# Expert weights in pieces of two experts with longer rows per partition, and TensorE working on two pieces at a time

## What is computed

```
for each layer of two:                       # w_gate, w_up: [16, 1024, 512], w_down: [16, 512, 1024]
    scores  = softmax(modulated(x) @ w_router)          # 256 tokens x 16 experts
    for each expert e:
        chosen = its 32 best tokens
        h      = silu(xs @ w_gate[e]) * (xs @ w_up[e])  # xs: the 32 chosen tokens, [32, 1024]
        y      = h @ w_down[e]                          # [32, 1024]
        x[chosen] += gate * weight * y
```

## Time and profile before

| | |
|---|---|
| runs | 1672.56, 1678.06, 1679.40 us; median 1678.06 |
| span of the profiled execution | 1675.7 us (its own time beside the span is not listed; the runs lie from 3.1 below to 3.7 above this span) |
| TensorE busy | 1557.6 us, 93% of the span |
| VectorE, ScalarE busy | 695.0 us, 347.3 us |
| HBM read | 438.51 MB, 262 GB/s over the span |
| mean granted TensorE clock | 0.979 of full |

### The profile page before, as it was taken

The page is one execution under the profiler, slowest core; times in us unless marked ns, Lnnn a source line. Parts: engine busy times, 40 slices in busy tenths (PEclk is TensorE's granted clock), DMA queues, the critical chain, the costliest instruction groups (busy, mean ns, idle before and its releaser), DMA issues.

```text
span 1675.7 us, 22597 instructions
## 1 busy us (share of the span) xinstructions
PE 1557.6 (93%) x9541; PEld 1123.0 (67%) x9541; DVE 695.0 (41%) x1635; ACT 347.3 (21%) x811; POOL 96.6 (6%) x113
## 2 busy tenths in 40 slices
PE   6998999999999999999999999999999999996656
PEld 3785788888776788888887878744544776842212
DVE  2334377777416378877433134402212334310011
ACT  3144310000114330010124243310010334211100
POOL 0003200000002310000011102000000002000000
PEclk8999999999999999999999999899999999998988
DMA  9568579996583268669363244499999444789997
GB/s 354 175 232 284 207 278 352 344 341 244 195 241 124 86 219 310 233 247 335 127 226 111 73 151 178 175 403 409 409 409 397 174 151 168 283 349 409 409 409 306
DMA packets 167705, 441.02 MB, mean 263 GB/s; under 512 B 7690, under 2 KB 19636, under 8 KB 167604
## 3 DMA queue, kind: packets, MB, share of 16 engines
q1 hardware_dynamic: 166800, 439.12, 70.4%
q10 hardware_dynamic: 804, 0.45, 0.1%
HBM read 438.51 MB, written 1.05 MB: 262 GB/s over the span
## 4 chain that ended last, share of the span: by engine, by line
PE 77%; DMA 11%; issue 3%; ACT 3%; POOL 2%; PEld 1%; DVE 1%; SPq 1%; ACTq 0%; PEldq 0%; DVEq 0%
PE bank L688 74%; DMA ring<-in_w_down 4%; DMA scr<-in_w_gate 3%; DMA ring<-in_w_up 3%; PE bank L699 2%; POOL scr L2424 2%; PEld bank L688 1%; DMA ring<-in_l_mod_w 1%; SPq L621 1%; PE bank L744 1%; ACT scr L2027 0%; ACTq L2189 0%; ACT hT L1965 0%; ACT brow L1982 0%; DVE scr L2491 0%
## 5 line engine op out<-in xcount | busy, mean ns | idle before, releaser
L688 PE MATMUL bank<-hT,ring 128*128 128x256 f32 (+1 forms) x2416 | 477.8, 383 | 4.9 <-ACT hT L1965 3.8
L688 PEld LDWEIGHTS bank<-hT,ring 128*128 128x128 f32 (+1 forms) x2416 | 384.3, 177 | 83.5 <-issue 11.9
L688 PE MATMUL bank<-scr,ring 128*128 128x256 f32 (+3 forms) x1764 | 378.4, 377 | 2.0 <-DVE mods L2590 1.1
L688 PEld LDWEIGHTS bank<-scr,ring 128*128 128x128 f32 (+2 forms) x1764 | 311.9, 186 | 54.9 <-issue 9.8
L2572 DVE SCALAR_TENSOR_TENSOR scr<-scr,csil 128x512 f32<-128x512 f32 x420 | 293.6, 752 | 3.2
L688 PE MATMUL bank<-scr 128*32 128x512 f32 (+8 forms) x1504 | 202.6, 427 | 15.7 <-ACT scr L2392 3.8
L688 PE MATMUL bank<-ring,scr 128*32 128x512 f32 (+2 forms) x1408 | 179.7, 588 | 19.9 <-DMA ring<-in_w_down 13.6
L688 PEld LDWEIGHTS bank<-scr 128*32 128x32 f32 (+4 forms) x1504 | 123.8, 153 | 89.3 <-issue 74.0
L688 PEld LDWEIGHTS bank<-ring,scr 128*32 128x32 f32 (+2 forms) x1408 | 68.2, 118 | 121.0 <-issue 87.7
L2424 POOL TENSOR_SCALAR scr<-scr,small 128x256 f32<-128x256 f32 (+2 forms) x88 | 79.8, 926 | 1009.5 <-DVE small L2627 855.1
L1993 ACT ACTIVATE scr<-bank 128x256 f32<-128x256 f32 x44 | 16.9, 384 | 376.8 <-PE bank L688 376.8
(11 more groups left out here) (307 smaller groups left out, 1085.6 us busy)
## 6 DMA issues: line engine op xcount, KB each, us to landing
ring<-in_w_down SPq DMA_DIRECT2D x25, 2048.0 KB, 23.8
scr<-in_w_ada SPq DMA_DIRECT2D x23, 2048.0 KB, 9.5
ring<-in_w_gate SPq DMA_DIRECT2D x23, 2048.0 KB, 15.5
scr<-in_w_up SPq DMA_DIRECT2D x19, 2048.0 KB, 22.7
scr<-in_l_mod_w SPq DMA_DIRECT2D x14, 2048.0 KB, 15.7
ring<-in_w_up SPq DMA_DIRECT2D x13, 2048.0 KB, 16.4
ring<-in_l_mod_w SPq DMA_DIRECT2D x10, 2048.0 KB, 12.0
ring<-in_l_ffn_wg SPq DMA_DIRECT2D x10, 2048.0 KB, 13.6
```

What stands on the lines that cost most here:

```text
L688: ins = nc.tensor.matmul(out, lhsT, rhs, start=start, stop=stop, skip_group_check=True)
```

## The change

Each expert piece now holds two experts instead of four and twice as many rows of each: for w_gate and w_up 512 rows, four neighbouring ones (8 KB) to a partition; for w_down 256 rows, two neighbouring ones (8 KB) to a partition. Its size stays 2 MB. Pieces 2k and 2k + 1 hold the same rows of experts 0, 1 and of experts 2, 3, and TensorE takes both before it starts on either, since its four column groups work on the four experts in turn. Both slots are released at the end of the pair. The w_down pieces of the last group of the last layer stay as they were.

The channel order follows: `gather` takes every fourth channel (a step of 16 bytes), `turn` of `hid` takes every second column (a step of 8 bytes) except in the last group of the last layer, and the columns of scale and shift for the last layer are built for four rows (16 small products in place of 8, after one more small copy on VectorE, in `mixers_last`).

```diff
             if kind < 2:
-                return w.rearrange("(g e) (s p two) n -> g s p e (two n)", e=GE, p=P, two=2)[group, s]
+                return w.rearrange("(g h e) (s p r) n -> g s h p e (r n)", e=2, h=2, p=P, r=4)[group, s // 2, s % 2]
             if in_halves(layer, group):
                 ...
-            return w.rearrange("(g e) (s p) n -> g s p e n", e=GE, p=P)[group, s]
+                return w.rearrange("(g e) (s p) n -> g s p e n", e=GE, p=P)[group, s]
+            return w.rearrange("(g h e) (s p r) n -> g s h p e (r n)", e=2, h=2, p=P, r=2)[group, s // 2, s % 2]
...
-            def shift_and_pairs():
+            def shift_and_rows():
...
-                for two in range(2):
-                    for hi in range(2):
-                        o = MODO[3] + (3 * 8 + hi) * 2
-                        for kind, cols in enumerate((acol[:, 64 + hi:64 + hi + 7:2], mods[:, o:o + 13:4])):
-                            mm(b[hi * HD:(hi + 1) * HD, NE + 8 * two + 4 * kind:NE + 8 * two + 4 * kind + 4],
-                               ident[:, two:P:2], cols, start=False, stop=True,
-                               signal=pe_to_dve if two and hi and kind else None)
+                for r in range(4):
+                    for q in range(4):
+                        mm(b[32 * q:32 * q + 32, NE + 4 * r:NE + 4 * r + 4], ident[:, r:P:4],
+                           acol[:, 64 + q:64 + q + 13:4], start=False, stop=True,
+                           signal=pe_to_dve if r == 3 and q == 3 else None)
...
-                                cols = slice(256 * (2 * half + c // 2) + c % 2, 256 * (2 * half + c // 2 + 1), 2)
+                                cols = slice(512 * half + c, 512 * (half + 1), 4)
...
-                        for s4 in range(4):
-                            if layer and kind == 0 and s4 == 2:
+                        for half in range(2):
+                            if layer and kind == 0 and half:
                                 pe.wait_ge(xs_ready, n["xs"])
-                            w = use(("moe", layer, kind, g, s4)).rearrange("p (e s n) -> p e s n", e=GE, s=2)
-                            for c2 in range(2):
-                                c = 2 * s4 + c2
+                            ws = [use(("moe", layer, kind, g, 2 * half + h)).rearrange("p (e r n) -> p e r n", e=2, r=4)
+                                  for h in range(2)]
+                            for r in range(4):
+                                c = 4 * half + r
                                 for i, s in enumerate(streams):
                                     for j in range(GE):
-                                        last = c2 == 1 and i == ns - 1 and j == GE - 1
+                                        last = r == 3 and i == ns - 1 and j % 2
                                         mm(banks[2 * s + kind][32 * j:32 * j + 32, :],
-                                           xs[s][:, c, 32 * j:32 * j + 32], w[:, j, c2, :], start=(c == 0),
-                                           stop=(c == DC - 1), signal=slots_released if last else None)
+                                           xs[s][:, c, 32 * j:32 * j + 32], ws[j // 2][:, j % 2, r, :],
+                                           start=(c == 0), stop=(c == DC - 1),
+                                           signal=slots_released if last else None)
...
-                            turn(banks[2 * s][:, f * P:(f + 1) * P], hid[s][:, f * P:(f + 1) * P],
+                            cols = slice(f * P, (f + 1) * P) if in_halves(layer, g) \
+                                else slice(2 * P * (f // 2) + f % 2, 2 * P * (f // 2 + 1), 2)
+                            turn(banks[2 * s][:, f * P:(f + 1) * P], hid[s][:, cols],
                                  hid_turned if f == 3 else None)
...
-                    for f in range(4):
-                        w = use(("moe", layer, 2, g, f)).rearrange("p (e n) -> p e n", e=GE)
+                    for f2 in range(2):
+                        ws = [use(("moe", layer, 2, g, 2 * f2 + h)).rearrange("p (e r n) -> p e r n", e=2, r=2)
+                              for h in range(2)]
+                        for r in range(2):
+                            f = 2 * f2 + r
...
+                nc.vector.tensor_copy(ac(9, 0, 8), mod(3, 3, 0, 8))
```

More of the change, by code:

```diff
@@ L178, in program @@
         mods = sb("mods", 48 * 6)
-        acol = sb("acol", 72)
+        acol = sb("acol", 80)
         csil_ = sb("csil", DC * 32)
@@ L475, in program @@
         scaled_router = routing[:, 0:DC * 32].rearrange("p (c e) -> p c e", c=DC)
-        shifted_logits, pair_cols = routing[:, 256:272], routing[:, 272:288]
+        shifted_logits, row_cols = routing[:, 256:272], routing[:, 272:288]
         token_roots, expert_sums = routing[:, 288:290], routing[:, 304:320]
@@ L1631, in beside @@
                     fourier_channels(dftd)
-                    shift_and_pairs()
+                    shift_and_rows()
                 attend(1, 2 * T, beside)
@@ L1801, in experts @@
                         return
-                    for f in range(4):
-                        w = use(("moe", layer, 2, g, f)).rearrange("p (e n) -> p e n", e=GE)
[L1804 to L1812, removed]
-                                       signal=slots_released if last else None)
+                    for f2 in range(2):
[3 more added lines that the diff above has]
+                            f = 2 * f2 + r
+                            for i, s in enumerate(streams):
+                                if f == 0:
+                                    pe.wait_ge(hid_copied, halves_ + g * ns + i + 1)
+                                for half in range(2):
+                                    for j in range(GE):
+                                        last = r == 1 and half == 1 and i == ns - 1 and j % 2
+                                        mm(banks[4 + 2 * s + half][32 * j:32 * j + 32, :],
+                                           hidT[s][:, f, 32 * j:32 * j + 32],
+                                           ws[j // 2][:, j % 2, r, half * 512:(half + 1) * 512],
+                                           start=(f == 0), stop=(f == 3),
+                                           signal=slots_released if last else None)
                     pe.drain().then_inc(y_ready, 1)
@@ L2366, in take_gathered @@
                             for c in range(4):
-                                at = 8 * (c % 2) + 2 * half + c // 2
+                                at = 4 * c + half
                                 ins = nc.scalar.activation(xs[s][:, 4 * half + c, :], b[:, c * P:(c + 1) * P],
-                                                           ACT.Identity, scale=pair_cols[:, at:at + 1],
-                                                           bias=pair_cols[:, at + 4:at + 5])
+                                                           ACT.Identity, scale=row_cols[:, at:at + 1],
+                                                           bias=row_cols[:, at + 2:at + 3])
                             ins.then_inc(xs_ready, 1)
```

## The result

Four executions of each kernel, side by side: before 1675.31 us in the median (1672.21 to 1679.40), after **1705.51 us** (1704.89 to 1705.61). The ratio is 1.017, with a 95% interval of 1.0151 to 1.0188: the medians differ by **30 us, slower**. That difference is some 2 us too large: two of the four runs before took 1672 us and two 1678 to 1679, while the later comparisons, with 17 to 29 runs of the kernel before each, have medians of 1677.3 to 1678.0, which would make it 27.5 to 28.2. The profiled execution has a span of 1703.6 us, 27.9 more than before, and its own time is 1705.43.

A forecast was written before the change was run, and what follows sets the result against it. TensorE was taken to bound the first layer and DMA only the last. Terms -4.8 + 1.8 + 3.5 + 0.2 + 0.3 + 0.1 = +1.1 us on 1678.1 gave 1679 us, range 1672 to 1710.

The forecast's parts named there:

- the likeliest case: Whole kernel: the summed terms hold, giving 1679 us with an own range of 1672 to 1687; chance 0.47.
- rival 1: Gather on TensorE: a step of 16 bytes doubles a load's time, giving 1709.5 us; chance 0.30, 0.20 in full.
- The step of 16 bytes: Gather on TensorE: 288 instructions on the path each cost 12 ns more, +3.5 us (0 to +34).
- Rows of 8 KB: Last layer's expert stream: 416 to 425 GB/s, 33 pieces gain 0.147 us each, -4.8 us (-3.0 to -6.5).
- Rival 2: Expert transfers: rows of 8 KB move no faster than 4 KB, giving 1684 us; chance 0.08.
- The late start: Last layer's stream: its first issue waits until the first pair's end, where both slots are released, +1.8 us.
- The first layer's cover: First layer's expert stream: pieces still land before TensorE needs them, with 6.7 us of margin, so no cost.
- The turn of `hid`: First layer: 32 loads get a step of 8 bytes at 6 to 9 ns each, +0.2 us.
- Scale and shift columns: Beside the last attention: 16 matmuls of 32 columns in place of 8 of 64, +0.3 us (0 to +0.7).
- VectorE's extra copy: Scale and shift columns: one more small copy of 8 columns, +0.1 us.
- The last pair of w_up: Last layer's end: w_down products start 8.3 to 10 us after this pair lands; 0 us taken, up to +2.
- Rival 4: Waiting for two pieces: last w_up pair at slow clock, +2, and an unseen wait, 1681 to 1688 us; chance 0.05.

The follow-up runs named there:

- The probe: Kernel before with first-layer gathers at steps of 4, 12, 32 and 20 bytes, last-layer moving operand at 8, 12 and 16 bytes; 1695.15 us, one run.
- pairs alone: Kernel before, rows still 4 KB, with TensorE waiting for two pieces and releasing both at the pair's end; 1679.84 us, ratio 1.0006.
- the sorted version: Changed kernel with ScalarE writing the tokens sorted by row, so the gather reads neighbouring columns; 1672.58 us, ratio 0.9972; again 1675.77 us, ratio 0.9978.
- the sorting alone: Kernel before with tokens sorted by row as ScalarE writes them, rows still 4 KB, no pairs; 1675.85 us, ratio 0.9981.
- the version sorted in pairs: Changed kernel with ScalarE writing sorted tokens, each channel beside its neighbour, so the gather has a step of 8 bytes; 1677.70 us.

## Why the prediction was wrong at its likeliest, and right in its range

The median lies in the range, but not in the likeliest case (1672 to 1687): rival 1 happened, for which the text gave 1709.5 us and a chance of 0.20 in full. Its difference was 31.4 us; 30.2 was measured. That the range held is no merit of the sum, which had +1.1 us; the text gave 0.64 to a change too small to be told. The range was stretched up to rival 1's time.

- **The step of 16 bytes** was the term that failed: 12 ns an instruction, +3.5 us. The trace shows four gathers 15.21 - 7.82 = 7.39 us longer and one 7.73 - 4.04 = 3.69 longer: **+33.3 us**, 115 ns an instruction, near the upper bound of 118. The count (288 on the path) was right, as the run with the step in the last layer only supports. What went wrong was the extrapolation: that 8 bytes cost 6 ns was taken for the start of a steady growth. The probe shows that it is the last point at which the instruction's own floor of 0.11 us still hides the reading. Behind it the cost rises by 57 ns for 4 bytes more. The observation under rival 1, that the spacing hardly exceeds the load and "there is no slack to hide in", was the stronger argument and got the lower weight.
- **Rows of 8 KB**: 421 GB/s, in the range of 416 to 425, and -4.3 us of stream for -4.8. Runs of 8 KB do not reach more than those of 7 KB had (423). Rival 2 is out: the rate rose at once, and only with the longer runs.
- **The late start**: 3.67 - 1.98 = 1.7 us for 1.8, and the same 3.67 with pairs alone.
- **The first layer's cover**: it held; no DMA is among TensorE's releasers there. In the changed kernel that tests little, as TensorE is 7.4 us slower in each group and the pieces land earlier than needed. In the sorted version, where TensorE is not slowed, it held as well.
- **The turn of `hid`**: 1.11 against 1.04 us for eight instructions, 9 ns each, +0.3 for 0.2.
- **Scale and shift columns**: 32 instructions end within 0.67 us, as the 16 of before: 0 for 0.3. 32 columns in each of four column groups cost no more than 64 in two. VectorE's extra copy, taken at 0.1, did not show on the path.
- **The last pair of w_up**: its products start at 1672.46, the turn at 1679.40 and the w_down products at 1681.03, 8.6 us behind the landing (8.3 to 10 was the text's). The last landing is at 1693.25, and the tail 10.4 us: nothing had to wait. Rival 4 is out.

The terms as measured, 33.3 - 4.3 + 1.7 + 0.3, make +31.0. The profiled executions differ by 27.9, and so do the medians, within 0.4, if the kernel before is taken at its 1677.3 to 1678.0 of more runs; the 30.2 of four runs each comes near the 31.0 by luck. The 3.1 between are hardly of the change: the first gather starts 0.5 us earlier (1075.81 for 1076.27), the store of the output is 0.9 shorter, and 1.6 lie in one group of 8 products behind the scale and shift columns, alike in both kernels, which ran at a lower granted clock before (0.64 in the mean from 1405.9 to 1410.6) and not after (1.00 from 1435.3 to 1438.4). TensorE's timeline, before and after:

```profile
1405.90 4.68 PE L688 MATMUL bank<-scr 128*128 128x512 f32 x8 [0.46 <-DVE routing L2969]
```

```profile
1435.33 3.04 PE L689 MATMUL bank<-scr 128*128 128x512 f32 x8 [0.48 <-DVE routing L2976]
```

## What to carry to other kernels

When a layout is changed so that DMA gets longer rows, look for who reads with the step that this makes: for 4-byte data, a step of two elements cost TensorE's operands 5% or less, a step of four doubled a 128-column product. Put the reordering where an engine with time writes the data anyway; that version beats the kernel before (ratios 0.9972 and 0.9978, neither interval reaching 1), though by 0.3% only, and how much of that is due to the longer rows and how much to the sorting alone (0.9981, up to 1.0000) the times don't tell. And where a small cost stands just at the point at which something else hides it, the next step can't be extrapolated from it.

## What the runs showed of the hardware

- A 128-column float32 operand of TensorE is read at about 1.8 ns for each 16-byte piece touched, nearly alike as the stationary (0.233 us at a step of 16 bytes) and as the moving one (0.227), as long as that is more than the 0.11 us that the instruction takes anyway.
- This reading does not go with TensorE's clock: the changed kernel's first gather, at a mean granted clock of 0.80 from 1075.81 to 1092.00, took the same 15.21 us as the others at 1.00, and so did that of the kernel before with the step of 16, at 0.89. With a step of 8 bytes the lower clock did count (5.36 for 4.04).
- ScalarE's copy of 128 x 512 from PSUM, reading neighbours and writing each element 512 bytes from the one before, lasts 1.06 us in the mean (0.94 to 0.96 from one to the next) in place of 0.59. Written in pairs of neighbours, as in the version sorted in pairs, it lasts 0.62.
- 128 x 2 runs of 8 KB moved at 421 GB/s, 128 x 4 runs of 4 KB at 409. In the last layer's full stream a piece of long runs was in the queue 32 to 38 us from issue to landing, where the kernel before has 23.6 to 29.0: SP got further ahead, with no gain from it.
- 80 of 93 runs of one kernel lie at 1669.8 to 1670.6 or at 1673.9 to 1677.7 us of span, so a change of 2 to 4 us in a program of 1675 is seen in the trace (the stream's length varies by 0.4 us over all profiles with one row length) and not in a median of a dozen runs.
